# Turned squares of a feed-forward block exchanged through GpSimd's queue instead of SyncE's

## What is computed

```python
def _swiglu(h, w_gate_up, w_down):
    gu = jnp.einsum('bsd,df->bsf', h, w_gate_up)
    g, u = gu[..., :FF], gu[..., FF:]
    return jnp.einsum('bsf,fd->bsd', jax.nn.silu(g) * u, w_down)      # FF = 2816, D = 1024

def first_block(...):
    for layer in range(DEPTH):
        h = h + _mixer(_rmsnorm(h, norm_mix[layer]), ...)
        h = h + _swiglu(_rmsnorm(h, norm_ffn[layer]), w_gate_up[layer], w_down[layer])
```

## Time and profile before

| | |
|---|---|
| median of 3 runs | 1984.82 us (1982.17 to 1985.72) |
| profiled execution | 1986.01 us |
| its span | 1984.2 us |
| mean granted clock of TensorE | 0.995 |
| bytes moved | 394.40 MB, mean 199 GB/s |

### The profile page before, as it was taken

The page is one execution under the profiler, slowest core; times in us unless marked ns, Lnnn a source line. Parts: engine busy times, 40 slices in busy tenths (PEclk is TensorE's granted clock), DMA queues, the critical chain, the costliest instruction groups (busy, mean ns, idle before and its releaser), DMA issues.

```text
span 1984.2 us, 25199 instructions
## 1 busy us (share of the span) xinstructions
PE 1931.4 (97%) x9363; PEld 1665.0 (84%) x9363; DVE 1269.7 (64%) x1853; ACT 1107.6 (56%) x1682; POOL 36.3 (2%) x60
## 2 busy tenths in 40 slices
PE   8999999899999999999999999999999999999999
PEld 7888888788888888888787888887888788888887
DVE  6576675665767666666667765756566566666654
ACT  6576544455765545644567666545544465565443
POOL 0000100000000000000000000000000000000000
PEclk9999999999999999999999999999999999999999
DMA  7555677755556878577764345777677664545775
GB/s 256 165 159 170 187 230 228 229 181 170 167 168 192 246 229 268 187 233 220 249 173 146 120 160 159 228 230 237 204 226 243 220 196 135 173 149 169 231 224 193
DMA packets 331082, 394.40 MB, mean 199 GB/s; under 512 B 22188, under 2 KB 225152, under 8 KB 330960
## 3 DMA queue, kind: packets, MB, share of 16 engines
q1 hardware_dynamic: 328880, 387.37, 62.4%
q0 software_dynamic: 2080, 5.41, 0.9%
HBM read 374.34 MB, written 18.36 MB: 198 GB/s over the span
## 4 chain that ended last, share of the span: by engine, by line
PE 60%; DMA 15%; SPq 9%; DVE 8%; ACT 5%; issue 3%; DVEq 0%; POOL 0%; ACTq 0%
PE M L820 18%; PE M L822 17%; PE M L821 17%; SPq L1759 5%; DVE WL L1325 4%; SPq L1779 3%; ACT WH L1101 2%; DMA RAW<-in_ffn_w_out 2%; DMA squares<-HC1b 2%; DMA squares<-HC0b 2%; DMA squares<-HD0b 2%; PE AUX L862 2%; DMA squares<-HB0b 2%; DMA RAW<-in_ffn_w_in 2%; DMA squares<-HD1b 1%
## 5 line engine op out<-in xcount | busy, mean ns | idle before, releaser
L1325 DVE TENSOR_TENSOR WL<-RAW,WH 128x1024 fp32r<-128x1024 f32 x669 | 812.1, 1218 | 492.7 <-ACT WH L1101 487.7
L1101 ACT ACTIVATE WH<-RAW 128x1024 fp32r<-128x1024 f32 x669 | 703.6, 1054 | 490.9 <-PE M L822 293.8
L820 PE MATMUL M<-WH,Bh 128*128 128x512 f32 x1792 | 694.8, 388 | 6.4 <-DVE WL L1325 6.3
L821 PE MATMUL M<-WL,Bh 128*128 128x512 f32 x1792 | 680.4, 380 | 0.0
L822 PE MATMUL M<-WH,Bl 128*128 128x512 f32 x1792 | 680.4, 380 | 0.0
L820 PEld LDWEIGHTS M<-WH,Bh 128*128 128x128 f32 x1792 | 339.6, 190 | 57.6 <-DVE WL L1325 9.6
L822 PEld LDWEIGHTS M<-WH,Bl 128*128 128x128 f32 x1792 | 339.4, 189 | 48.4
L821 PEld LDWEIGHTS M<-WL,Bh 128*128 128x128 f32 x1792 | 339.9, 190 | 44.0
L1130 ACT ACTIVATE AS<-M,KEEP 128x256 f32<-128x256 f32 x132 | 54.7, 465 | 28.6 <-PE M L822 23.3
L820 PE MATMUL M<-WH,MTh 128*128 128x512 f32 x128 | 53.6, 419 | 0.0
L862 PE MATMUL AUX<-CC,X 128*128 128x128 f32 x192 | 33.4, 304 | 20.6 <-DVE X L1383 15.5
(11 more groups left out here) (411 smaller groups left out, 2485.9 us busy)
## 6 DMA issues: line engine op xcount, KB each, us to landing
RAW<-in_ffn_w_in SPq DMA_DIRECT2D x352, 256.0 KB, 3.9
RAW<-in_w_in SPq DMA_DIRECT2D x104, 512.0 KB, 3.6
RAW<-in_w_gate_up SPq DMA_DIRECT2D x176, 256.0 KB, 4.1
RAW<-in_ffn_w_out SPq DMA_DIRECT2D x88, 512.0 KB, 5.2
RAW<-in_w_down SPq DMA_DIRECT2D x44, 512.0 KB, 5.1
RAW<-in_x_w_kv SPq DMA_DIRECT2D x32, 512.0 KB, 3.5
RAW<-in_even_w_in SPq DMA_DIRECT2D x24, 512.0 KB, 3.9
RAW<-in_odd_w_in SPq DMA_DIRECT2D x24, 512.0 KB, 3.8
```

The lines of the kernel that those rows point to most:

```text
L820: e.matmul(out, s.hi, wh, start=s.at0, stop=False)
L821: e.matmul(out, s.hi, wl, start=False, stop=False)
L1101: e.activation(p.WH[:, h, 0:s.size], p.RAW[:, i, 0:s.size], ACT.Copy).then_inc(k.w_hi, 1)
L1325: e.tensor_tensor(p.WL[:, h, 0:s.size], p.RAW[:, s.u % NRAW, 0:s.size], hi.bitcast(F32), ALU.subtract).then_inc(k.w_lo, 1)
```

## The change

The squares' transfers leave SyncE's list and become two kinds of steps, `sq_out` at the chunk's end + 1.0 and `sq_in` at the end + 3.0, which GpSimd issues in its list. Their waits are the same. The split of the rows that come back moves from 8.6 to 12.6 steps behind the end of its chunk.

```diff
@@ Plan.ffn
-            x = self.add("hx", c.end + 8.6)
+            x = self.add("hx", c.end + 12.6)
+            for kind, at in (("sq_out", 1.0), ("sq_in", 3.0)):
+                self.add(kind, c.end + at).x = x
@@ gpsimd
+        elif s.kind == "sq_out":
+            n = s.x.n
+            if s.x.f.past is not None:
+                e.wait_ge(k.d_hx[n % 2], 64 * ((n - 1) // 2))
+            e.wait_ge(k.blocked, 2 * n)
+            e.dma_start(p.parked[n % 2].rearrange("c (p e) -> p c e", p=P),
+                        s.x.f.squares.rearrange("p (c e) -> p c e", c=4)).then_inc(k.d_hb[n % 2], 16)
+        elif s.kind == "sq_in":
+            n = s.x.n
+            if s.x.f.past is not None:
+                e.wait_ge(k.hx_lo, s.x.f.past.n)
+            e.wait_ge(k.d_hb[n % 2], 16 * ((n + 1) // 2))
+            for c in range(4):
+                e.dma_start(s.x.f.x[32 * c:32 * c + 32, :].rearrange("p (q e) -> p q e", q=4),
+                            p.parked[n % 2, c].rearrange("(q j e) -> j q e", q=4, e=P)).then_inc(k.d_hx[n % 2], 16)
@@ sync
-    out = [s for s in p.for_pe if s.kind == "hx"]
-    back = list(out)
     for i in range(3, len(p.units)):
-        while out and out[0].f.c.done + NRAW + NHL <= i:
-            squares_out(out.pop(0))
-        while back and back[0].f.c.done + NRAW + NHL + 1 <= i:
-            squares_in(back.pop(0))
         weights(i)
```

More of the change, by code:

```diff
@@ L1761, in weights @@
             e.dma_start(dst.rearrange("p (k n) -> p k n", k=kn), src).then_inc(k.raw[s], 16)
[L1763 to L1780, removed]
     e.dma_start(p.CC[:, 0:P], a["c0"][:, 0:P]).then_inc(k.d_ident, 16)
@@ L1789, in sync @@
     e.dma_start(p.C1[:, 1536:2048], a["c1"][:, 1536:2048]).then_inc(k.d_cs, 16)
-    out = [s for s in p.for_pe if s.kind == "hx"]
-    back = list(out)
     for i in range(3, len(p.units)):
-        while out and out[0].f.c.done + NRAW + NHL <= i:
-            squares_out(out.pop(0))
-        while back and back[0].f.c.done + NRAW + NHL + 1 <= i:
-            squares_in(back.pop(0))
         weights(i)
-    assert not back
     for s in p.outs:
```

## The result

The changed kernel takes 1950.78 us (median of 4 runs, 1949.62 to 1953.81) against 1984.72 for the kernel before, measured beside it (4 runs): 33.9 us less. The ratio is 0.9833, with a 95% interval of 0.9816 to 0.985. The forecast was 1955 us, 1949 to 1977.

What follows compares the result with a forecast made beforehand. SyncE's queue, standing for the squares, was taken to starve TensorE of weights. Down stages 27.0 us plus about 4 in gate/up gave a ceiling of 31, less 1 for gaps: 1984.8 - 30 = 1955 us, range 1949 to 1977.

Steps and rivals of the forecast that it cites:

- The bound: Gate/up stages: SyncE's queue, standing for squares, delivers weights late; the lead shrinks 1.0 to 1.3 us a chunk, starving TensorE.
- part 1: SyncE in gate/up loses about 5.7 us a chunk, keeps 5.2 in 10.4, and is no bound.
- part 2: Gate/up weight buffer round: 7.5 to 8.5 us; the unit behind the eviction about 10.3 to 11.3, against TensorE's 10.4.
- the good end: Low side of the range for the weight unit behind the eviction, about 10.3 us: its round slips by nothing.
- part 3: GpSimd takes over the squares' issues at 0.55 us each, 0.94 the largest: 2.7 to 4.7 us in 10.4 a chunk.
- part 4: Returned rows arrive after 15.9 us (low 13.2, high 23.8), the split's turn at 16.6; ScalarE's 27 us of waiting go or shrink.
- part 5: Down projection needs the last split by step 20; at 12.6 over six steps, 8 us, are left: no cost.
- part 6: DMA traffic: same bytes in less time, gate/up needing about 250 GB/s, which the engines can deliver.
- The sum: Four down stages 27.0 us, gate/up about 4: ceiling 31, less 1 for gaps that stay.
- part of the gain: Rival, 0.15: squares and weights compete on the 16 engines, the weights' round stays near 11.3 us; 1965 to 1975.
- nothing: Rival, 0.08: GpSimd's rows arrive about 2 us late, SyncE's freedom is spent in ScalarE's wait; 1981 to 1989.
- The exchange is slower through GpSimd: Rival, 0.12: rows come after 16.6 us, ScalarE waits and conversions slip; 5 to 10 us per block, 2015 us.

Runs made afterwards that it cites:

- Run 1: Kernel before with only the split moved from 8.6 to 12.6, SyncE still exchanging the squares at the old places: 1978.27 us, ratio 0.997.
- run 3: Kernel before with the split at 12.6 and SyncE issuing the squares' way back two weight units later: 1953.0 us, ratio 0.9845.
- run 9: Changed kernel with the split at 8.6 and one small extra transfer, with its wait, ahead of each way back: 2041.37 us, ratio 1.0298.
- run 2: Changed kernel with the split back at 8.6, so only the queue differs from the kernel before: 1953.0 us, ratio 0.9842.
- run 5: Kernel before with the split at 12.6 and SyncE's way back three weight units later: 2019.96 us, ratio 1.0174.
- run 6: Kernel before with the split at 12.6 and SyncE's way back four weight units later: 2188.42 us, ratio 1.1029.
- run 7: Kernel before with the split kept at 8.6 and SyncE's way back two weight units later: 2129.14 us, ratio 1.0731.
- run 10: Changed kernel with GpSimd issuing each way back at 9.5 steps, behind the next chunk's way out: 2074.44 us, ratio 1.0468.
- run 11: Changed kernel with the split at 6.6, ahead of the next chunk's eviction on ScalarE: 2213.73 us, ratio 1.1173.
- run 4: Kernel before with the split at 12.6 and the exchange left out, the split reading the turned squares directly: 1952.81 us, ratio 0.9842.
- run 8: Changed kernel with each way out issued twice by GpSimd, the second to a tensor nobody reads: 1952.53 us, ratio 0.9835.

## Why the prediction was right, step by step

*The bound.* Right, and shown by runs 1 and 3: the weights were late since SyncE stood still for the squares' landing. Run 1 parts it from ScalarE's wait, run 3 from the issues and the traffic, which are all there in it. How fast the lead drains was mis-sized: I had read one cycle, 11.7 us, where the stage's distances go from 9.3 to 12.0 with a mean of 10.96. That is 0.6 us a chunk over TensorE's 10.36, about 6 us in the third block's stage, and not 11 to 14. The forecast's time came from the down stages' lengths and not from this drain, so the error didn't reach it.

*SyncE, part 1.* Right. *The weights' round, part 2.* I took the good end; loads of that tensor land in 3.7 us (median over the span), and TensorE has no wait for weights in a feed-forward block.

*GpSimd's issues, part 3.* 0.55 for one piece was right (2.18 for four); the way out takes 0.76. The table's store made no wait at the split.

*Does the data arrive, part 4.* The split's turn at 16.6 us was exact. The way was mis-sized, to the safe side: 15.9 forecast and 13.2 as the low bound, some 11.8 measured. Most of it is the way out: I had added 1.2 us to SyncE's 5.8, and it took 3.3. That the 5.8 held time behind the weight loads issued just before on the same queue fits two runs (4.2 in run 3 with the loads spread; 6.2 in run 9 on GpSimd's queue, 1 us behind its own four loads), but no run parts this from the load on the DMA engines. Eviction and turn took 879.56 - 876.85 = 2.7 us where I had 3.5. The way back took 3.9, where I had put 3.2; SyncE's took 3.3 in run 3, outside the stall, so little of that is GpSimd's. So the split at 12.6 had 4.7 us to spare, and run 2 shows that 8.6 would have done.

*The later split costs nothing, part 5; traffic, part 6.* Right; the first block's gate/up stage now moves 253 GB/s at full granted clock.

*The sum.* The down stages: 27.0 forecast, 66.7 + 64.7 + 63.8 + 65.0 - 4 x 58.2 = 27.4 measured. Gate/up stages: 4 forecast; two of them went from 116.6 to 115.7 and from 117.3 to 115.2, and the first block's, from its first to its last matmul, from 140.5 to 138.3, together 5.2. Span to span it is 1984.2 - 1949.5 = 34.7, where I had 30, and 31 as the ceiling. Of the missing 4.7, 0.4 and 1.2 are these, 1 is the gaps that I left in and that went too, 0.6 the last block's down stage, which I hadn't counted. 1.6 lie in a stage that the change doesn't touch, read from the stages' windows, here of the changed kernel:

```profile
1640.60:1678.60 38.00, 35.45 (x180) 30.09 (x179) 30.07 (x53) 23.97 (x40) 0.00 (x0) 1.00 0.46 153
```

Before it took 39.6 us at a mean granted clock of 0.96. Those 1.6 us are chance and no part of the change: a drop of the clock at that place comes and goes from trace to trace, with the change and without it (last section). They belong to the two profiled executions; the 33.9 us between the medians needn't hold them.

*The rivals.* Neither "part of the gain" nor "nothing" came: all four down stages are at 58.2 us. "The exchange is slower through GpSimd" did not happen; runs 5 to 7 and 9 to 11 show that its mechanism is real and that I had priced it too low: in run 5, with some 3 us more of ScalarE's waiting a chunk than before the change, it costs 35 us against the kernel before, not nothing, since the wait closes a ring through the issuing queue. Neither the lock between VectorE and GpSimd's transfers (the Trainium skill, SBUF — State Buffer, "SBUF: two separate sides") nor its reverse showed itself: GpSimd's issues stayed at 0.76 and 2.18 us and L1327 at 1218 ns. The Trainium skill, DMA: Bandwidth & Descriptors, "Issuing engines are not separate DMA queues", holds that another issuer saves only the issuing engine's time for the issue. The runs agree as far as the transfers go: with the waiting gone, run 3 reaches 1953.0 us on one queue. What GpSimd's queue saved SyncE was mainly a wait, 3.4 us a chunk, and not issue time.

## What to carry to other kernels

Add up one period of each in-order queue, its waits included: issues, the wait for a transfer of its own to land, and what stands between. If it is over the bound engine's period, the lead drains at the difference and the loss shows up only a stage later; issuing the dependent transfer a few entries later can be as good a cure as another queue. Here two units later was (run 3), and three was worse than no change (run 5). So before moving a wait later, follow what its end releases: if that leads back to the issue that it waits for, each microsecond over the period is paid every time round.

## What the runs showed of the hardware

A 256 KB store of squares landed in 5.8 us on SyncE's queue right behind six weight loads, in 4.2 there when the loads were spread (run 3), in 3.3 on GpSimd's queue in the changed kernel, and in 6.2 on GpSimd's queue close behind four loads of its own (run 9). The 64 KB loads back took 2.0 us on SyncE's queue in the stall, 3.3 there in run 3 and 3.9 on GpSimd's. The same store on the same queue so landed up to 2.9 us later with other transfers under way.

By either queue the exchange took the same share of the 16 DMA engines' time. The two queues' shares together are 66.9% of the span in run 3, 66.8% in the changed kernel and 60.0% in run 4 without it. The packets of the whole run are fewer with GpSimd's queue, 271945 against 331082, for the same 394.4 MB. The gate/up loads of 256 KB landed in 3.3 us without the exchange (run 4), 3.7 with it and 4.1 with the way out doubled (run 8); the time was the same in all three.

The same idle gap of TensorE in the same place (2.28 us, ahead of L876 in the kernel before) is in all traces. In the 7.6 us from the matmul behind it, the mean granted clock is 0.78 in the kernel before and in runs 1, 3, 4, 5, 8 and 11, with matmuls 0.43 us apart, at 1.2 GHz. It is 1.00 in the changed kernel and in runs 2, 6, 7, 9 and 10. The drop doesn't follow from the gap's length alone, and it doesn't go with the change.
